# Two 32-byte tiles moved from the end of the right-hand stack of SBUF to the middle of the left-hand one

## The reference

```
h   = RMSNorm(x)
z   = h @ W_in                      # pool | q | k | v | forget
mix = concat[PoolMixer(z_pool), ForgettingAttention(q, k, v, f)] @ W_out
x   = x + mix
x   = x + PEER(RMSNorm(x))          # 8 heads, product keys 2 x 128, top 16
```

## Time and profile before

| | |
|---|---|
| median of three runs | 1458.82 us (1458.24 to 1458.92) |
| the profiled execution, its own time | 1458.24 us |
| its span, first to last instruction | 1456.4 us |
| mean granted clock of TensorE | 0.999 |
| busy: PE, PEld, DVE, ACT, POOL | 1442.4, 1283.5, 1136.5, 569.6, 982.0 us |
| DMA | 381.57 MB, mean 262 GB/s |

### The profile page before, as it was taken

How to read it: one execution, slowest core, us unless ns; L and a number is a source line. 1 busy time by engine, 2 the same in 40 slices (tenths; PEclk the granted TensorE clock), 3 DMA queues, 4 the chain that set the end, 5 groups by cost and what they waited for, 6 DMA issues and landing times.

```text
span 1456.4 us, 20488 instructions
## 1 busy us (share of the span) xinstructions
PE 1442.4 (99%) x7591; PEld 1283.5 (88%) x7591; DVE 1136.5 (78%) x1867; ACT 569.6 (39%) x789; POOL 982.0 (67%) x534
## 2 busy tenths in 40 slices
PE   9999999999999999999999999999999999999998
PEld 6766788889999999999999999988888888888887
DVE  5588661469999999499999998497777777677775
ACT  5565344233333333444444444333333333333332
POOL 4432334446787788876666665598888788878883
PEclk9999999999999999999999999999999999999999
DMA  5321123225788878988999995999888888888883
GB/s 209 111 93 60 59 87 137 81 79 182 225 269 276 267 258 279 334 298 315 360 366 357 358 343 192 360 389 359 315 342 346 345 324 332 346 346 338 319 306 117
DMA packets 122293, 381.57 MB, mean 262 GB/s; under 512 B 11768, under 2 KB 28408, under 8 KB 122240
## 3 DMA queue, kind: packets, MB, share of 16 engines
q1 hardware_dynamic: 70384, 202.69, 39.3%
q0 software_dynamic: 36864, 134.23, 25.2%
q10 hardware_dynamic: 14992, 44.06, 7.6%
HBM read 336.89 MB, written 44.06 MB: 262 GB/s over the span
## 4 chain that ended last, share of the span: by engine, by line
PE 94%; DVE 3%; ACT 2%; issue 1%; DMA 1%; SPq 0%; DVEq 0%; ACTq 0%
PE bank L695 28%; PE bank L696 28%; PE bank L697 28%; PE bank L922 6%; PE bank L854 1%; DVE pr L1173 1%; ACT pr L550 1%; PE bank L825 0%; PE wide L695 0%; PE wide L696 0%; PE wide L697 0%; DVE pad L1123 0%; PE bank L935 0%; DMA vec<-vecs_dram 0%; DMA nf<-forget_dram 0%
## 5 line engine op out<-in xcount | busy, mean ns | idle before, releaser
L448 POOL TENSOR_TENSOR wl<-raw,wh 128x1024 fp32r<-128x1024 f32 x210 | 512.6, 2443 | 300.9 <-ACT wh L478 298.5
L695 PE MATMUL bank<-hh,wh 128*128 128x384 f32 (+1 forms) x1184 | 416.9, 352 | 0.2 <-DVE hl L1139 0.2
L696 PE MATMUL bank<-hl,wh 128*128 128x384 f32 (+1 forms) x1184 | 406.4, 343 | 0.0
L697 PE MATMUL bank<-hh,wl 128*128 128x384 f32 (+1 forms) x1184 | 406.4, 343 | 0.0
L695 PE MATMUL bank<-wh,Wh 128*128 128x512 f32 x768 | 298.9, 389 | 0.0
L697 PE MATMUL bank<-wh,Wl 128*128 128x512 f32 x768 | 298.8, 389 | 0.0
L696 PE MATMUL bank<-wl,Wh 128*128 128x512 f32 x768 | 298.8, 389 | 0.0
L478 ACT ACTIVATE wh<-raw 128x1024 fp32r<-128x1024 f32 (+1 forms) x217 | 228.2, 1052 | 148.3 <-PE bank L697 136.5
L695 PEld LDWEIGHTS bank<-hh,wh 128*128 128x128 f32 x1184 | 222.8, 188 | 8.1 <-issue 0.7
L696 PEld LDWEIGHTS bank<-hl,wh 128*128 128x128 f32 x1184 | 222.7, 188 | 7.6 <-issue 0.7
L697 PEld LDWEIGHTS bank<-hh,wl 128*128 128x128 f32 x1184 | 222.2, 188 | 7.6
(11 more groups left out here) (182 smaller groups left out, 1652.3 us busy)
## 6 DMA issues: line engine op xcount, KB each, us to landing
raw<-uT_dram SPq DMA_DIRECT2D x128, 512.0 KB
xraw<-v_dram SPq DMA_DIRECT2D x72, 512.0 KB
raw<-v_dram SPq DMA_DIRECT2D x56, 512.0 KB
a_dram<-act_a ACTq DMA_DIRECT2D x64, 384.0 KB
wf<-a_dram SPq DMA_DIRECT2D x32, 768.0 KB, 6.9
raw<-wst_dram SPq DMA_DIRECT2D x40, 512.0 KB
gates_dram<-gbuf ACTq DMA_DIRECT2D x32, 512.0 KB
gt<-gates_dram SPq DMA_DIRECT2D x32, 512.0 KB
```

The source lines that it names most:

```text
L448: pool.tensor_tensor(wl[:, n % SPLIT, :], raw_of(n), wh[:, n % SPLIT, :].bitcast(F32), ALU.subtract).then_inc(w_lo, 1)
L695: pe.matmul(dst, ah, bh, start=start, stop=False)
L696: pe.matmul(dst, ah, bl, start=False, stop=False)
L697: return pe.matmul(dst, al, bh, start=False, stop=stop)
```

## The change

The stack `edge` at the end of SBUF is gone. Its two tiles are taken in `mixers` instead, between `rcol` and `rrec`. Nothing else is changed.

```diff
@@ -97,10 +97,6 @@
         vec = sb("vec", [P, N_VEC])
         keys = sb("keys", [P, 2, NKEY])
         identr = sb("identr", [P, P], F32R)
-
-        edge = ExitStack()
-        rmin = sb("rmin", [P, TB, 2], F32, edge, "right")
-        rsum = sb("rsum", [P, TB, 2], F32, edge, "right")
 
         dense = ExitStack()
         x = sb("x", [P, KD, T], F32, dense, "right")
@@ -140,6 +136,8 @@
         pm = sb("pm", [P, T], where=mixers)
         newt = sb("newt", [P, T], where=mixers)
         rcol = sb("rcol", [P, TB], where=mixers)
+        rmin = sb("rmin", [P, TB, 2], where=mixers)
+        rsum = sb("rsum", [P, TB, 2], where=mixers)
         rrec = sb("rrec", [P, TB, 2], where=mixers)
         wp = sb("wp", [P, 4, P], where=mixers)
         mixers.close()
```

## The result

The changed kernel takes 1467.39 us (median of six runs, 1466.82 to 1468.42), the one before 1458.38 in the runs beside it: 1.0063 times as long, with a 95% interval of 1.0053 to 1.0074. That is 9.0 us slower, where no measurable change was forecast.

What follows compares the result with a forecast made beforehand. TensorE was taken to bound the kernel, busy 1442.4 of 1456.4 us. All terms were 0, adding nothing to the profiled 1458.24 us; the median of three runs, 1458.8 us, was forecast, range 1456.8 to 1460.8.

Steps and rivals of the forecast that it cites:

- term (2): Moved `Wh1` and `Wl1`, stationary in half of 2304 matmuls: longer loads hide under matmuls, 0; without that cover 0.6 us.
- Term (1): Moved `hh` and `hl` as moving operand of L695 to L697, 3552 matmuls: 0 ns each, bound 1.8 us either way.
- Terms (3) to (5): Loads into moved tiles; `rmin`, `rsum`, `rrec` in the attention (bound 0.6 us); `wp` in the pool products: 0 each.
- A: PE's reads of moved `hh` and `hl` at L695 to L697 get longer, 0.83 ns each: 1461.8 us; chance 0.03.
- Its sign: In the profile after, the L695 to L697 groups a ns or more longer than 352, 343, 343, all of `mh` unchanged.
- B: DMA loads into moved tiles (`xraw`, `gt`, `wf`) take 2% longer and PE waits for all: 1462.9 us; chance 0.03.
- C: VectorE and GpSimd collisions fall otherwise, mostly 60 to 285 us: 1454.6 or 1463.0 us; chance 0.04, half each side.
- D: Allocator rounds the 64 bytes away, so nothing moves: 1458.8 us; counted within the 0.90 for no measurable change.

Runs made afterwards that it cites:

- e4: Kernel before with only `Wh1` and `Wl1` moved, 192 bytes lower (`N_VEC = 64` makes the room): 1466.09 us, 1.0050.
- e3: Changed kernel with a spare of 64 bytes ahead of `raw`, so left-hand tiles from `raw` on move up 64 bytes too: 1457.89 us, 0.9995.
- e1: Changed kernel with a 64-byte spare ahead of `Wh1`, putting `Wh1` and `Wl1` back in place while the other right-hand tiles stay moved: 1459.28 us, 1.0008.
- e2: Kernel before with `rmin` and `rsum` in `mixers`, but a 64-byte spare at the right-hand stack's end so no large tile moves: 1458.58 us, 1.0001.
- e8: Kernel before with both slots of `Wh` and `Wl` 192 bytes lower, 64 higher in steps of 256: 1474.00 us, 1.0108.
- e6: Kernel before with `wh` and `wl` 192 bytes lower (`N_VEC = 32`; `raw`, `keys` and `identr` 384 lower): 1474.29 us, 1.0114.

## Why the prediction was wrong

**The step that failed** is term (2), "a nanosecond more of a load hides under the matmul before it: 0, and without that cover 1152 x 0.5 ns = 0.6 us". It measured 8.0 us with the spill (after, and e4, where no other right-hand tile moves), more than ten times its bound. The load's own row did not change in either, 187/188/192 ns, so the error was to take that row as the whole price: the load does lie beside a matmul, but the step from one matmul to the next grew from 226.7 to 233.3 ns.

**What let it through** is the reading of the earlier trace rows: "So the step is 0 ns for a read by PE". The row of `newt` is a matmul whose moving operand stands 96 past a multiple of 128 beside a stationary operand in `cst`. It spoke of one address in one pairing and I took it for all. By their addresses, moreover, neither `newt` nor `sq` stood at distance 0 to its stationary operand: they are at +32 and -32 in steps of 256, whose costs in the down phase are alike (6.8 and 6.7 ns), so two dear pairings may have been compared with each other. e3 shows that the question was put wrongly: with the operands of the three lines all 96 past, nothing is lost. The question that should have been asked of each matmul is whether its two operands still stand to each other as before: in the kernel before those of L695 to L697 all stood at distance 0 in steps of 256, and after the change two groups of them no longer do.

**Term (1)**, the moving `hh` and `hl`, was given 0 with a bound of 1.8 us. It is inside: 0.8 us in the queries (e1 keeps it, 1459.28), at -64, the cheap side, and nothing in the 384-column form. But its bound held by the shapes alone: by the starts the 512-column form grew by 2.1 ns, beyond the 0.5 ns that bounded it, and the term is small only because most of the 3552 matmuls have 384 columns; 384 are in the queries with 512. The comparison of 334 ns from either stack in the earlier trace rows was of two aligned pairs and so could not show it.

**Terms (3) to (5)**: 0 each within what the runs can tell, as predicted. e2 tests `rmin`, `rsum`, `rrec` and `wp` (1.0001), e1 the transfers (1.0008).

**The rivals.** A had the right engine, and matmuls that take longer for an address, but the wrong operand: it looked at `hh` and `hl` alone, 3552 matmuls and 1461.8 us, and e1, which keeps them moved, is at 1459.28. Its sign came true all the same, 354, 345 and 345 ns with `mh` unchanged, in the changed kernel and in e1: a reader who went by it would have blamed `hh` and `hl`. B would have given 1462.9 us and is excluded by e1, which has all the moved transfers and is at 1.0008 (0.9998 to 1.0017). Of its argument one reading was off: the 241.9 and 150.6 us of the earlier trace rows are waits until `Wl` and `wl` have been written, and the slots that they are made from are free, not until they are read. C did not happen: PE's idle time is 14.4 us, against 14.0, and e1 takes 8.1 us away without touching VectorE's or GpSimd's work. D is excluded by the time itself.

**The price of the evidence.** The three lines had distance 0 in the kernel before, where the tiles of these lines have sizes that are multiples of 256 bytes and it was the 64 bytes of `rmin` and `rsum` that brought the right-hand stack into step with the left-hand one (`x` ends at 229280, 160 past a multiple of 256); the rows of before could show 226.7 ns for 512 columns but no second value to compare. What they could have shown is that no stationary operand in the three lines stood off its moving one anywhere, so that the case had no row, and the bound for a thing without a row was taken from the printing of a number instead of from the length of the operation. One cycle at 2.4 GHz in each of 1152 steps is 0.5 us; the 6.6 ns of the step are 16 of them, and no row excluded that.

**What stays open** is how the engine comes by it. The runs show a dependence on the distance of the two operands in steps of 256 bytes, with its sign, and that neighbouring steps grow too. The Trainium skill, in SBUF — State Buffer, section "Who interferes with whom", gives the engine two read ports, one for the moving operand and one for weight loads, and calls them independent; by that the distance would be worth nothing, and e8 measured 15.3 us for it, so here the measurement decides.

## What to carry to other kernels

A change of the memory plan is a change of the program: after moving a tile of any size, list which operands stand on the same stack behind it, and for each heavy matmul compare the addresses of its stationary and its moving operand in steps of 256 bytes before and after. In this kernel a spare of 64 bytes in the place of the two tiles (e2) makes the same change free. When an operation is hidden beside another in the profile, its own duration doesn't tell what it costs; measure from start to start of what it lies beside. The same holds for matmuls that overlap: here 2 ns more of recorded duration in 2976 of them cost nothing, and 3 ns more in the down phase stood for 8.0 us.

## What the runs showed of the hardware

With the granted clock at 1.00, a 512-column matmul of these fp32 parts started every 226.7 ns when its two operands stood at distance 0 in steps of 256 bytes, and every 229 to 235 ns at the six other distances tried, -64 being the cheapest (2.2 ns) and +96 the dearest (8.0 ns); the distances ±32, 128 and +96 were measured in one run each. In the 384-column form -64 cost nothing (4.16 us for 24 in both) and +64 some 1.3 to 1.8 ns (4.19 or 4.20 us for 24 in e6). Moving both operands by 64 bytes did not matter (e3), nor did the kernel's time show transfers into tiles at a new phase of 256 bytes (e1, where PE waits for none of them).
